# The scan of a state-space block: decay rows from a DRAM scratch instead of spreading products on TensorE

## The chip, the cores and the metric

The kernel runs on one core of a Trainium2 chip. The metric is the time of the whole kernel on the device, in microseconds (us). The median of three runs before the change is 1635.37 us (1634.31 to 1642.18).

## The reference, cut to what matters

The program is a transformer-like layer pair, then a second block whose mixer is a two-directional state-space scan (SSD), and a mixture of experts. The change touches only the scan of the second block. Sequence length is 256 and there are 32 heads of width 64, 4 groups, 128 states, 2 directions. For each head and direction:

```python
acs = jnp.cumsum(ac, axis=1)                     # running sum of the log decays
seg = acs[:, :, None] - acs[:, None, :]
decay = jnp.exp(jnp.where(lower, seg, -jnp.inf)) # 0 above the diagonal
cb = jnp.einsum('bign,bjgn->bijg', cc, bc)
y_diag = jnp.einsum('bijg,bijgr,bjgrp->bigrp', cb, decay, xc)
y_off = jnp.einsum('bign,bgrpn->bigrp', cc, state) * jnp.exp(acs)[..., None]
```

The kernel needs, for every head and direction, a tile in which each partition j holds the whole row acs[i] over i. To it the mask (0 or a large negative number) is added, acs[j] is subtracted as the bias of an exponential, and the result is multiplied by dt and by `cb`.

## The kernel before, in words

Every engine has its own program, written out by hand in its own order: `tensor` (PE), `scalar` (ACT), `vector` (DVE), `gpsimd` (POOL), `sync` (SP). Semaphores join them: `at(key)` names a point that another engine signals. All weights stream through a ring in SBUF. SP loads a *unit* (two column blocks of 512 KB); a unit is used as two *quarters*. For each quarter ACT makes a rounded high part (`hi_to`, 128x1024), POOL or DVE then the low part (`lo_to`), and PE multiplies high and low parts (three matmuls for each product). `split_done` says that PE has used a quarter up. In this part of the kernel the ring has two slots: before SP may load a unit it waits until both quarters of the unit two before it have their `hi` and `lo` (`load`, called by `load_to`).

The scan has 32 steps, `steps = [(c, d) ...]`: c is a pair of heads (0 to 15), d a direction; step n belongs to c = n // 2, d = n % 2. In the loop over n:

- PE: `spread(n + 2)`, `projected(n)` (the product of quarter n of the `merged` weights, 24 matmuls), `head_out(n)` (needs `mb` of step n), and in some steps `carried` (the state's part, in 12 of the steps) and `c_by_b`. `spread` makes the rows of two heads in PSUM: a product with a selection matrix (384 columns) and one with the identity that adds the mask (256 columns), for each of two heads.
- ACT: `hi_to(q0 + n + 4)`, which makes the high part of quarter n + 3; `exps(n + 2)`; at odd n `normed` (the last output's square and scaling); `gate_kept`.
- DVE: `weights_of(n + 1)` (four operations, signals `mb`); at even n `summed` and `gated`, at odd n `low`; then `carried`.
- POOL: `lo_to(q0 + n + 4)`; at odd n `squares`; sometimes a `carried` sum. All low parts of these quarters are POOL's.
- SP: nothing but units, each as early as the ring lets it. The unit with quarters n + 4 and n + 5 (n even) takes the slot of the unit with quarters n and n + 1.

The convolution ahead of the scan makes the running sums (`acs`), which PE transposes; ACT and DVE store them rounded as high and low parts (`ACSR`). ACT also makes a rounded copy of identity, selection matrix and masks (`KR`).

Of the kernel before, what the change touches and what calls it, by code (L numbers as in the profile page):

```python
# [6 lines left out]
F32 = mybir.dt.float32  # L7
F32R = mybir.dt.float32r
I32 = mybir.dt.int32
ALU = mybir.AluOpType  # L10
# [3 lines left out]
P = 128  # L14
D = 1024
# [16 lines left out]

CST = [("ident", 128), ("selh", 64), ("negf", 256), ("negb", 256), ("ones", 128), ("tle", 128), ("tge", 128), ("tlt", 128), ("tgt", 128),
       ("invf", 32), ("iota", 128), ("selbc", 128), ("selc", 2), ("half", 128)]
# [11 lines left out]
def constants():  # L46
# [6 lines left out]
    i = np.arange(256)[None, :]  # L53
    c["selh"] = p % 64 == np.arange(64)[None, :]
    c["negf"] = np.where(i % 128 >= p, 0.0, NEG)
# [236 lines left out]
def program(nc, A, out):  # L292
    st = ExitStack()
    with st:
# [35 lines left out]
        ar_r = rounded_at("arena_r", 25472, ar_at)  # L330
        acs_r = rounded_at("acs_r", 384, rows_at + 4 * 4 * D)
        ps = st.enter_context(nc.psum_tensor("ps", [P, 8, 512], F32))
# [39 lines left out]
        s_last = {e: sem(f"last_{e}") for e in ("dve", "pool")}  # L372
        s_w = [[sem(f"expert{i}") for i in range(9)]] + [[sem(f"expert{r}_{i}") for i in range(8)] for r in range(1, ROUNDS)]
        s_second = [sem(f"expert_second{i}") for i in range(4)]
        s_round = [None] + [{e: sem(f"round{r}_{e}") for e in ("pe", "act", "dve")} for r in range(1, ROUNDS)]
# [80 lines left out]
        AA = view(19712, 4, 64)  # L456
        ACS = view(19712, 2, 128)
        NACS = view(19968, 2, 64)
        WCE = view(20096, 4, 64)
        WC, EAC = WCE[:, 0:2, :], WCE[:, 2:4, :]  # L460
        ACSR = acs_r[:, :]
        H0T = XC
# [5 lines left out]

        KR = rounded_at("kr_r", 704, rows_at + 4 * 3 * D)[:, :]
        identr, selr, negr = KR[:, 0:128], KR[:, 128:192], [KR[:, 192:448], KR[:, 448:704]]  # L470
        SACC = view(17088, 1, 256)[:, 0, :]
        ED = [view(20480 + 768 * i, 2, 384) for i in range(3)]
        YO = [view(22784, 2, 512), view(23808, 2, 512)]
# [126 lines left out]
        def tensor(t):  # L600
# [346 lines left out]
            def convolution():  # L947
# [17 lines left out]
                for m in range(24):  # L965
# [16 lines left out]
                    if m == 11:  # L982
                        bk = take(("acst",), ("acsr", 0), ("acsr", 1))
                        t.wait_ge(*at("acs"))
                        for i in range(4):
                            made = t.transpose(bk[:, tok(i)], ACS[:, i % 2, :], ident)
                        made.then_inc(*sig(s_turn, ("acst_t",)))
# [58 lines left out]
            def scan():  # L1046
# [14 lines left out]

                def spread(n):
                    c, d = steps[n]
                    for e in range(2):
                        col = d * 32 + 2 * c + e
                        bk = take(("sp", n, e), ("ex", n, e))
                        t.wait_ge(*at("kr"))
                        t.wait_ge(*at("acsr", 0))
                        t.wait_ge(*at("acsr", 1))
                        t.matmul(bk[:, 0:384], selr[:, col:col + 1].to_broadcast([P, P]), ACSR, True, False)  # L1070
                        t.matmul(bk[:, parts_in[d][2]], identr, negr[d], False, True).then_inc(*sig(s_mm, ("sp", n, e)))

                def head_out(n):
# [7 lines left out]
                    for x, (cols, o) in enumerate(((early, slice(0, 256)), (late, slice(128, 256))) if d == 0 else ((late, slice(0, 256)), (early, slice(0, 128)))):  # L1081
                        for e in range(2):
                            h = 2 * c + e
                            made = t.matmul(bk[64 * e:64 * e + 64, o], XL[:, x if d == 0 else 1 - x, h * 64:h * 64 + 64], ED[n % 3][:, e, cols], d == 0 and x == 0, False)
                    made.then_inc(*sig(s_mm, ("ho", n)))
# [7 lines left out]
                    drop(("y", c))  # L1093

                c_by_b(0)
                spread(0)
                state_sum(3)
                for d in range(2):
                    for i in range(2):
                        carried(0, d, i)  # L1100
                    if d == 0:
                        spread(1)
                for n in range(32):
                    g, x = divmod(n, 8)
                    if x == 0 and g:
                        drop(("cb", g - 1))
                    if n + 2 < 32:
                        spread(n + 2)
                    if n >= 2:
                        projected(n)  # L1110
                    head_out(n)
                    if g < 3 and 2 <= x < 6:
                        carried(g + 1, *divmod(x - 2, 2))
                    if g < 3 and x == 6:
                        c_by_b(g + 1)
                drop(("cb", 3))

# [280 lines left out]
        def scalar(s):  # L1398
# [222 lines left out]
            def convolution():  # L1621
# [26 lines left out]
                for m in range(24):  # L1648
# [15 lines left out]
                    if m == 11:  # L1664
                        s.wait_ge(*at("acst_t"))
                        for z in range(4):
                            rs = slice(32 * z, 32 * z + 32)
                            made = s.activation(ACSR[rs, :], B("acst")[rs, 0:384] if z % 2 else B("acst")[rs, 128:512], ACT.Copy)
                        made.then_inc(*sig(s_act, ("acsr", 0)))
                    if m == 16:  # L1670
                        for h in range(2):
                            s.wait_ge(*at("ga", 3, 1, h))
                        s.wait_ge(*at("cst"))
                        s.activation(KR, cst[:, 0:704], ACT.Copy).then_inc(*sig(s_act, ("kr",)))
                    if m in KEPT:
# [20 lines left out]
            def scan():  # L1696
                q0 = first["merged",][1]
                def exps(n):
                    c, d = steps[n]
                    late, early, _ = parts_in[d]  # L1700
                    if n == 0:
                        s.wait_ge(*at("tk", CHUNKS.index(15)))
                    if n >= 3:
                        s.wait_ge(*at("ho", n - 3))
                    for e in range(2):
                        col = d * 32 + 2 * c + e
                        bk = B("sp", n, e)
                        s.wait_ge(*at("sp", n, e))
                        s.activation(ED[n % 3][:, e, late], bk[:, late], ACT.Exp, bias=NACS[:, 1, col:col + 1])
                        s.activation(ED[n % 3][:, e, early], bk[:, early], ACT.Exp, bias=NACS[:, 0, col:col + 1]).then_inc(*sig(s_act, ("ex", n, e)))  # L1710

# [175 lines left out]
        def vector(v):  # L1887
# [412 lines left out]
            def convolution():  # L2300
# [5 lines left out]
                for m in range(24):  # L2306
# [23 lines left out]
                    if m == 10:  # L2330
                        v.wait_ge(*at("wc"))
                        v.wait_ge(*at("dts"))
                        for i in range(2):
                            v.copy(ACS[:, :, 64 * i:64 * i + 64], fold(B("dts")[:, 128:256], 2))
                        then(v.tensor_scalar(NACS, fold(B("dts")[:, 128:256], 2), -1.0, None, ALU.mult), ("acs",))
                        v.wait_ge(*v.latest)
                        then(v.tensor_tensor(WC, WC, DT[:, 0:2, :], ALU.mult), ("wc", "made"))
                    if m == 11:
                        v.wait_ge(*at("acsr", 0))
                        for z in (2, 3):  # L2340
                            rs = slice(32 * z, 32 * z + 32)
                            made = v.tensor_tensor(ACSR[rs, :], B("acst")[rs, 0:384] if z % 2 else B("acst")[rs, 128:512], ACSR[rs, :], ALU.subtract)
                        then(made, ("acsr", 1))
                    if m == 13:
# [26 lines left out]
            def scan():  # L2371

                def weights_of(n):
                    c, d = steps[n]
# [3 lines left out]
                    for e in range(2):  # L2378
                        col = d * 32 + 2 * c + e
                        v.wait_ge(*at("ex", n, e))  # L2380
                        for z, cols, w in ((3, late, cb_in[d][0]), (2, early, cb_in[d][1])):
                            x = ED[n % 3][:, e, cols]
                            made = v.stt(x, x, DT[:, z, col:col + 1], bk[:, w], ALU.mult, ALU.mult)
# [28 lines left out]
                def low(c):  # L2412
                    v.wait_ge(*at("xsh", c))
                    then(v.stt(XSL[:, c, :], XST[:, c, :], ghalf[:, c:c + 1], xsh(c), ALU.mult, ALU.subtract), ("xsl", c))

                weights_of(0)
                state_kept(3)
                gated(0)
                for d in range(2):
                    for i in range(2):  # L2420
                        carried(0, d, i)
                for n, (c, d) in enumerate(steps):
                    g, x = divmod(n, 8)
                    lo_to(first["merged",][1] + n + 4)
                    if n + 1 < 32:
                        weights_of(n + 1)
# [536 lines left out]
        def sync(y):  # L2963
# [44 lines left out]
            for l in range(2):  # L3008
# [5 lines left out]
                for m, u in ADA_AT[l].items():  # L3014
# [3 lines left out]
                    y.wait_ge(*at("am", u))  # L3018
                load_to(first["z", 1, 1][0] if l == 0 else n1)
            load_to(first["end",][0])  # L3020
            y.wait_ge(*at("o2", 1, 1, "kept"))
# [77 lines left out]
```

## Time and profile before

| | |
|---|---|
| median of three runs | 1635.37 us |
| the profiled execution, span from first to last instruction | 1635.8 us |
| granted TensorE clock, mean | 0.995 |
| PE / DVE / ACT / POOL busy | 97% / 47% / 37% / 29% |
| scan, from PE's first loop step to its last product | about 860 to 1015 us |

The profile lists what each engine did when. PE is matmul time, DVE the vector engine, ACT the activation engine, POOL the GpSimd engine, SPq SP's queue of transfers. The mean times of matmuls overlap, because they are pipelined: what one costs is read from the distance between starts. The profiled execution's own time is its span, 1635.8 us; the page shows nothing around it.

### The profile page before, as it was taken

The numbers are of one execution on the slowest core, as the hardware profiler recorded it, in microseconds if no ns is written. First come the engines' busy times: TensorE is split into PE (matmuls) and PEld (weight loads), VectorE is DVE, ScalarE is ACT, GpSimd is POOL, SyncE is SP. The second block draws the span as 40 slices with busy tenths as digits, with TensorE's granted clock in tenths as the row PEclk, the third lists the DMA queues.
The fourth block names the chain that finished last, engine by engine and source line by source line (L and its number), as shares of the span: only waits on it lengthen the run. The fifth ranks groups of instructions, "written<-read, shape, count | busy, mean of one in ns | idle before, by whom it ended". The sixth has DMA issues, their size and how long they took to land.

```text
span 1635.8 us, 24320 instructions
## 1 busy us (share of the span) xinstructions
PE 1585.8 (97%) x9881; PEld 1204.8 (74%) x9881; DVE 762.6 (47%) x1261; ACT 611.0 (37%) x1113; POOL 473.7 (29%) x305
## 2 busy tenths in 40 slices
PE   6999999999999999999999999999999999999997
PEld 5988899878889998888778888898644444444442
DVE  4554433246454332578776666446532323333223
ACT  4644444345544443555446665333211111111010
POOL 4342655433434444300036665343300000000000
PEclk9999999999999999999999999999999999999998
DMA  7654997546439986433313333957999999999995
GB/s 264 220 158 128 266 260 232 174 141 218 153 98 312 263 269 220 118 80 85 103 52 104 104 103 120 296 152 264 360 400 423 425 420 422 424 422 424 421 422 210
DMA packets 244757, 397.87 MB, mean 243 GB/s; under 512 B 6837, under 2 KB 195697, under 8 KB 223392
## 3 DMA queue, kind: packets, MB, share of 16 engines
q1 hardware_dynamic: 237840, 365.45, 64.6%
q10 hardware_dynamic: 3776, 20.85, 3.2%
q0 software_dynamic: 3024, 9.95, 1.8%
q8 instruction: 81, 1.33, 0.3%
q14 instruction: 36, 0.29, 0.1%
HBM read 395.17 MB, written 1.05 MB: 242 GB/s over the span
## 4 chain that ended last, share of the span: by engine, by line
PE 82%; DMA 9%; DVE 3%; issue 2%; ACT 2%; POOL 1%; ACTq 0%; DVEq 0%; POOLq 0%; SPq 0%
PE ps L145 80%; DMA arena<-in_w_expert_up 4%; DMA arena<-in_w_expert_gate 4%; PE ps L147 2%; DVE arena L151 1%; DVE arena L155 1%; DMA ring<-in_w_out 1%; POOL split_r L151 1%; ACT arena L149 1%; DMA X<-in_x 1%; ACT split_r L149 1%; DVE split_r L151 0%; DMA ring<-in_w_in 0%; POOL arena_r L151 0%; DVE X L155 0%
## 5 line engine op out<-in xcount | busy, mean ns | idle before, releaser
L145 PE MATMUL ps<-arena_r,split_r 128*128 128x256 f32 (+1 forms) x2984 | 459.9, 288 | 2.2 <-POOL split_r L151 2.2
L151 POOL TENSOR_TENSOR split_r<-ring,split_r 128x1024 fp32r<-128x1024 f32 (+1 forms) x142 | 329.3, 2320 | 304.2 <-ACT split_r L149 275.6
L145 PEld LDWEIGHTS ps<-arena_r,split_r 128*128 128x128 f32 x2984 | 393.3, 188 | 19.7 <-issue 13.6
L149 ACT ACTIVATE split_r<-ring 128x1024 fp32r<-128x1024 f32 (+1 forms) x293 | 295.7, 1019 | 265.2 <-PE ps L145 183.2
L151 DVE TENSOR_TENSOR split_r<-ring,split_r 128x1024 fp32r<-128x1024 f32 (+1 forms) x151 | 217.4, 1442 | 302.6 <-ACT split_r L149 302.4
L145 PE MATMUL ps<-split_r,arena_r 128*128 128x512 f32 (+1 forms) x1520 | 341.0, 378 | 4.1 <-POOL split_r L151 2.4
L145 PEld LDWEIGHTS ps<-split_r,arena_r 128*128 128x128 f32 x1520 | 276.1, 189 | 50.3 <-issue 7.1
L145 PE MATMUL ps<-arena 128*64 128x512 f32 (+8 forms) x1456 | 299.1, 461 | 6.3 <-DMA arena<-in_w_expert_gate 2.2
L145 PE MATMUL ps<-hhh_r,split_r 128*128 128x256 f32 (+1 forms) x976 | 221.7, 316 | 0.0
L145 PEld LDWEIGHTS ps<-arena 128*64 128x64 f32 (+2 forms) x1456 | 126.0, 148 | 129.7 <-issue 115.2
L145 PE MATMUL ps<-ring,arena 128*64 128x512 f32 (+2 forms) x768 | 211.4, 576 | 3.0 <-DMA ring<-in_w_expert_up 1.7
L149 ACT ACTIVATE arena<-ps 128x256 f32<-128x256 f32 (+4 forms) x175 | 75.4, 446 | 257.3 <-PE ps L145 215.3
L145 PEld LDWEIGHTS ps<-hhh_r,split_r 128*128 128x128 f32 x976 | 161.6, 188 | 12.5 <-issue 0.6
L151 DVE TENSOR_TENSOR arena<-arena,ps 128x512 f32<-128x512 f32 (+1 forms) x120 | 72.7, 634 | 202.9 <-PE ps L145 177.3
L145 PEld LDWEIGHTS ps<-ring,arena 128*64 128x64 f32 (+1 forms) x768 | 77.3, 144 | 98.8 <-issue 89.4
L171 POOL DMA_DIRECT2D rows<-in_ln_g x1 | 0.6, 617 | 412.2 <-PE ps L145 412.2
L149 ACT ACTIVATE arena<-ps,modc 128x128 f32<-128x128 f32 x80 | 30.0, 455 | 199.2 <-PE ps L145 198.5
L149 ACT ACTIVATE arena_r<-arena 128x512 fp32r<-128x512 f32 (+2 forms) x96 | 51.0, 540 | 138.5 <-DVE arena L155 86.9
L145 PEld LDWEIGHTS ps<-arena,X 128*128 128x128 f32 x640 | 77.4, 198 | 28.5 <-issue 26.4
L145 PE MATMUL ps<-arena,X 128*128 128x128 f32 x640 | 82.6, 284 | 14.6 <-DVE arena L153 14.6
L155 DVE SCALAR_TENSOR_TENSOR arena<-ps,rows,arena 128x508 f32<-128x508 f32 (+4 forms) x104 | 69.7, 675 | 28.5 <-ACT arena L149 21.9
L151 POOL TENSOR_TENSOR arena_r<-arena,arena_r 128x256 fp32r<-128x256 f32 (+1 forms) x46 | 38.1, 830 | 151.3 <-ACT arena_r L149 143.7
(164 smaller groups left out, 1234.0 us busy)
## 6 DMA issues: line engine op xcount, KB each, us to landing
ring<-in_w_gate_up SPq DMA_DIRECT2D x88, 512.0 KB, 7.4
arena<-in_w_expert_gate SPq DMA_DIRECT2D x15, 2048.0 KB, 27.9
ring<-in_w_in SPq DMA_DIRECT2D x57, 512.0 KB, 5.3
ring<-in_w_expert_gate SPq DMA_DIRECT2D x13, 2048.0 KB, 25.7
ring<-in_w_expert_down SPq DMA_DIRECT2D x13, 2048.0 KB, 28.5
arena<-in_w_ada SPq DMA_DIRECT2D x24, 1024.0 KB, 7.4
arena<-in_w_expert_up SPq DMA_DIRECT2D x12, 2048.0 KB, 25.1
ring<-in_w_down SPq DMA_DIRECT2D x22, 1024.0 KB, 4.9
```

The costliest lines, as they stand in the source:

```text
L145: made = e.matmul(*a, **k)
L147: made = e.transpose(*a, **k)
L149: made = e.activation(*a, **k)
L151: made = e.tensor_tensor(*a, **k)
L155: made = e.scalar_tensor_tensor(**k)
L171: made = e.dma_start(*a, **k)
```

## The change

The running sums, transposed, are written once to a DRAM scratch `decays` of 64 rows of 384 numbers (`ACST`, 32-bit numbers, no rounding parts). For each step SP loads two of these rows onto all 128 partitions (3072 bytes a partition, 393 KB) into one of four buffers. DVE adds the mask, which PE has put into a PSUM bank once; ACT takes the exponential in place. `spread`, `KR`, `selh` and the parts of `ACSR` are gone. A fourth `ED` buffer lies in `rows`.

```diff
 # PE
-                def spread(n):            # per head: select product 384 columns, mask product 256
+                def masks():
+                    bk = take(("mask",), ("mk", 31), hold=True)
+                    t.matmul(bk[:, 0:256], ident, C("negf"), True, True)
+                    t.matmul(bk[:, 256:512], ident, C("negb"), True, True).then_inc(*sig(s_mm, ("mask",)))
+                masks()
                 c_by_b(0)
-                spread(0)
                 for n in range(32):
-                    if n + 2 < 32:
-                        spread(n + 2)
 # ACT, convolution step 11, and exps
-                        for z in range(4):
-                            rs = slice(32 * z, 32 * z + 32)
-                            made = s.activation(ACSR[rs, :], B("acst")[rs, 0:384] if z % 2 else B("acst")[rs, 128:512], ACT.Copy)
+                        for d in range(2):
+                            rs = slice(32 * d, 32 * d + 32)
+                            made = s.activation(ACST[rs, :], B("acst")[rs, 0:384] if d else B("acst")[rs, 128:512], ACT.Copy)
+                        made.then_inc(*sig(s_act, ("acst", "kept")))
+                        s.wait_ge(*s.latest)
+                        s.dma_start(DECAYS, ACST).then_inc(*landed(s_decays, ("decays_out",)))
-                        s.activation(KR, cst[:, 0:704], ACT.Copy).then_inc(*sig(s_act, ("kr",)))
-                    if n >= 3:
-                        s.wait_ge(*at("ho", n - 3))
+                    s.wait_ge(*at("mk", n))
 # DVE
+                def masked(n):
+                    _, d = steps[n]
+                    x = ED[n % 4][:, :, parts_in[d][2]]
+                    v.wait_ge(*at("mask"))
+                    v.wait_ge(*at("ed", n))
+                    then(v.tensor_tensor(x, x, B("mask")[:, 256 * d:256 * d + 256].unsqueeze(1).to_broadcast([P, 2, 256]), ALU.add), ("mk", n))
+                masked(0)
                 weights_of(0)
                 state_kept(3)
                 gated(0)
+                masked(1)
                 for n, (c, d) in enumerate(steps):
                     lo_to(first["merged",][1] + n + 4)
+                    if n + 2 < 32:
+                        masked(n + 2)
                     if n + 1 < 32:
                         weights_of(n + 1)
 # SP
+            def decays(n):
+                c, d = steps[n]
+                if n == 0:
+                    y.wait_ge(*at("decays_out"))
+                elif n < 4:
+                    y.wait_ge(*at("silu", 23))
+                    y.wait_ge(*at("tk", CHUNKS.index(15)))
+                else:
+                    y.wait_ge(*at("ho", n - 4))
+                two = DECAYS[32 * d + 2 * c:32 * d + 2 * c + 2, :].rearrange("a b -> (a b)")
+                y.dma_start(EDR[n % 4], two.partition_broadcast(P)).then_inc(*landed(s_ed[n % 4], ("ed", n)))
+
+            load_to(first["conv20",][0])
+            decays(0)
+            for n in range(1, 32):
+                load_to(first["merged",][0] + (n + 4) // 2 + 1)
+                decays(n)
             load_to(first["end",][0])
```

## Rows read from the trace of the kernel before

**Rows 1.** Busy time in a stretch; columns: stretch, PE, PEld, DVE, ACT, POOL, clock, DMA share, GB/s.

```profile
860.30:1014.50 154.20, 154.20 (x1195) 133.50 (x1193) 97.85 (x199) 93.42 (x212) 93.14 (x52) 1.00 0.40 110
...
1160.00:1165.00 5.00, 3.07 (x20) 2.91 (x21) 3.27 (x19) 0.20 (x1) 0.00 (x0) 0.82 1.01 423
```

**Rows 2.** Timeline of PE, one spread between a head's products and the next projection.

```profile
937.66 0.42 PE L145 MATMUL ps<-acs_r,kr_r 128*128 128x384 f32 x1
...
937.92 0.28 PE L145 MATMUL ps<-kr_r 128*128 128x256 f32 x1
...
938.04 0.33 PE L145 MATMUL ps<-acs_r,kr_r 128*128 128x384 f32 x1
...
938.21 0.28 PE L145 MATMUL ps<-kr_r 128*128 128x256 f32 x1
...
938.33 0.28 PE L145 MATMUL ps<-hhh_r,split_r 128*128 128x256 f32 x1
```

**Rows 3.** Timeline of PE: two `carried`; then the heads' products of steps 29 to 31.

```profile
858.95 1.88 PE L145 MATMUL ps<-arena 128*128 128x512 f32 x4
860.26 0.74 PE L145 MATMUL ps<-acs_r,kr_r 128*128 128x384 f32 x1
...
1005.51 0.87 PE L145 MATMUL ps<-arena 128*64 128x256 f32 x8
...
1009.79 0.87 PE L145 MATMUL ps<-arena 128*64 128x256 f32 x8
1013.63 0.87 PE L145 MATMUL ps<-arena 128*64 128x256 f32 x8
1014.43 0.71 PE L145 MATMUL ps<-cst_sb,arena 128*128 128x128 f32 x4
```

**Rows 4.** Timeline of ACT, two steps: gate, high part, exponentials, square, scaling, gate, high part.

```profile
895.13 0.47 ACT L149 ACTIVATE arena<-ps,stat 128x256 f32<-128x256 f32 x1 [1.00 <-PE ps L145]
...
901.34 1.36 ACT L149 ACTIVATE arena<-ps,arena 128x256 f32<-128x256 f32 x4
902.57 0.43 ACT L149 ACTIVATE arena<-arena 128x256 f32<-128x256 f32 x1
902.87 0.52 ACT L149 ACTIVATE arena_r<-arena,stat 128x256 fp32r<-128x256 f32 x1
904.39 0.47 ACT L149 ACTIVATE arena<-ps,stat 128x256 f32<-128x256 f32 x1 [1.00 <-PE ps L145]
904.76 1.05 ACT L149 ACTIVATE split_r<-ring 128x1024 fp32r<-128x1024 f32 x1
```

**Rows 5.** Timeline of POOL: low parts; the first at the scan's start, the second in it.

```profile
856.69 2.36 POOL L151 TENSOR_TENSOR split_r<-ring,split_r 128x1024 fp32r<-128x1024 f32 x1 [5.86 <-ACT split_r L149]
...
896.63 2.40 POOL L151 TENSOR_TENSOR split_r<-ring,split_r 128x1024 fp32r<-128x1024 f32 x1 [2.08 <-ACT split_r L149]
```

**Rows 6.** SP's queue: issues of one unit (the second line from a later start), and their landing.

```profile
899.11 0.99 SPq L171 DMA_DIRECT2D ring<-in_w_in  x2
...
899.52 0.58 SPq L171 DMA_DIRECT2D ring<-in_w_in  x1
...
DMA to landing us min/median/max: 4.2/5.2/6.1
```

**Rows 7.** SP's waits ahead of its transfers between 850 and 1010 us.

```profile
SPq L138 <- ACT split_r L149: 112.3, 16, 15.8
SPq L138 <- POOL split_r L151: 36.6, 15, 2.6
```

**Rows 8.** Timeline of DVE in an even step: weights, sum, gating product, gate.

```profile
904.00 1.38 DVE L155 SCALAR_TENSOR_TENSOR arena<-arena,ps 128x256 f32<-128x256 f32 x4
905.84 0.48 DVE L155 SCALAR_TENSOR_TENSOR arena<-arena,stat,ps 128x256 f32<-128x256 f32 x1 [0.46 <-PE ps L145]
906.35 2.22 DVE L151 TENSOR_TENSOR arena<-arena 128x256 f32<-128x256 f32 x1
909.66 0.42 DVE L155 SCALAR_TENSOR_TENSOR arena<-arena,ps 128x256 f32<-128x256 f32 x1 [1.09 <-ACT arena L149]
```

**Rows 9.** DVE's two-input additions and products in the scan; ns min/median/max, first and last start.

```profile
L151 DVE TENSOR_TENSOR arena<-ps,arena x14: 690/692/694, 860.0 to 969.2; 128x512 f32<-128x512 f32 x14
L151 DVE TENSOR_TENSOR arena<-arena x14: 425/2214/2622, 865.9 to 998.3; 128x256 f32<-128x256 f32 x14
```

**Rows 10.** The page: a queue's packets, MB and share; transfers, count, KB, us to landing.

```profile
q0 software_dynamic: 3024, 9.95, 1.8%
...
rows<-in_g_mix_post POOLq DMA_DIRECT2D x2, 512.0 KB, 5.0
...
out<-arena SPq DMA_DIRECT2D x4, 256.0 KB, 2.3
```

More of the change, by code:

```diff
@@ L31 @@
 C1, C2, C3 = 6.25, 0.033185303211212158203125, 3.9683743e-09
-CST = [("ident", 128), ("selh", 64), ("negf", 256), ("negb", 256), ("ones", 128), ("tle", 128), ("tge", 128), ("tlt", 128), ("tgt", 128),
+CST = [("ident", 128), ("negf", 256), ("negb", 256), ("ones", 128), ("tle", 128), ("tge", 128), ("tlt", 128), ("tgt", 128),
        ("invf", 32), ("iota", 128), ("selbc", 128), ("selc", 2), ("half", 128)]
@@ L53, in constants @@
     i = np.arange(256)[None, :]
-    c["selh"] = p % 64 == np.arange(64)[None, :]
     c["negf"] = np.where(i % 128 >= p, 0.0, NEG)
@@ L330, in program @@
         ar_r = rounded_at("arena_r", 25472, ar_at)
-        acs_r = rounded_at("acs_r", 384, rows_at + 4 * 4 * D)
         ps = st.enter_context(nc.psum_tensor("ps", [P, 8, 512], F32))
@@ L373, in program @@
         s_w = [[sem(f"expert{i}") for i in range(9)]] + [[sem(f"expert{r}_{i}") for i in range(8)] for r in range(1, ROUNDS)]
+        s_decays, s_ed = sem("decays_out"), [sem(f"decay{i}_in") for i in range(4)]
         s_second = [sem(f"expert_second{i}") for i in range(4)]
@@ L456, in program @@
         AA = view(19712, 4, 64)
-        ACS = view(19712, 2, 128)
+        ACS = view(19712, 2, 64)
         NACS = view(19968, 2, 64)
@@ L460, in program @@
         WC, EAC = WCE[:, 0:2, :], WCE[:, 2:4, :]
-        ACSR = acs_r[:, :]
+        ACST = rows[0:64, 4 * D:4 * D + 384]
         H0T = XC
@@ L467, in program @@
         XW = view(24576, 2, 2, 512)
-        KR = rounded_at("kr_r", 704, rows_at + 4 * 3 * D)[:, :]
-        identr, selr, negr = KR[:, 0:128], KR[:, 128:192], [KR[:, 192:448], KR[:, 448:704]]
+        DECAYS = nc.dram_tensor("decays", (64, 384), F32).ap()
         SACC = view(17088, 1, 256)[:, 0, :]
-        ED = [view(20480 + 768 * i, 2, 384) for i in range(3)]
+        EDR = [view(20480 + 768 * i, 1, 768)[:, 0, :] for i in range(3)] + [rows[:, 2 * D:2 * D + 768]]
+        ED = [fold(x, 2) for x in EDR]
         YO = [view(22784, 2, 512), view(23808, 2, 512)]
@@ L982, in convolution @@
                     if m == 11:
-                        bk = take(("acst",), ("acsr", 0), ("acsr", 1))
+                        bk = take(("acst",), ("acst", "kept"))
                         t.wait_ge(*at("acs"))
                         for i in range(4):
-                            made = t.transpose(bk[:, tok(i)], ACS[:, i % 2, :], ident)
+                            made = t.transpose(bk[0:64, tok(i)], ACS[:, i % 2, :], ident)
                         made.then_inc(*sig(s_turn, ("acst_t",)))
@@ L1060, in carried @@
                     t.matmul(bk, CT[:, g, tok(i)], H0T[:, d, half(g)], True, True).then_inc(*sig(s_mm, ("yo", g, d, i)))
-                def spread(n):
[L1063 to L1071, printed above, removed]
+                def masks():
+                    bk = take(("mask",), ("mk", 31), hold=True)
+                    t.matmul(bk[:, 0:256], ident, C("negf"), True, True)
+                    t.matmul(bk[:, 256:512], ident, C("negb"), True, True).then_inc(*sig(s_mm, ("mask",)))
                 def head_out(n):
@@ L1083, in head_out @@
                             h = 2 * c + e
-                            made = t.matmul(bk[64 * e:64 * e + 64, o], XL[:, x if d == 0 else 1 - x, h * 64:h * 64 + 64], ED[n % 3][:, e, cols], d == 0 and x == 0, False)
+                            made = t.matmul(bk[64 * e:64 * e + 64, o], XL[:, x if d == 0 else 1 - x, h * 64:h * 64 + 64], ED[n % 4][:, e, cols], d == 0 and x == 0, False)
                     made.then_inc(*sig(s_mm, ("ho", n)))
@@ L1100, in scan @@
                         carried(0, d, i)
-                    if d == 0:
-                        spread(1)
                 for n in range(32):
@@ L1115, in scan @@
                         c_by_b(g + 1)
-                drop(("cb", 3))
+                drop(("cb", 3), ("mask",))
             def two_chunks(n, key, free, src):
@@ L1665, in convolution @@
                         s.wait_ge(*at("acst_t"))
-                        for z in range(4):
-                            rs = slice(32 * z, 32 * z + 32)
-                            made = s.activation(ACSR[rs, :], B("acst")[rs, 0:384] if z % 2 else B("acst")[rs, 128:512], ACT.Copy)
[L1669 to L1673, printed above, removed]
-                        s.activation(KR, cst[:, 0:704], ACT.Copy).then_inc(*sig(s_act, ("kr",)))
+                        for d in range(2):
[4 more added lines that the diff above has]
+                        s.dma_start(DECAYS, ACST).then_inc(*landed(s_decays, ("decays_out",)))
                     if m in KEPT:
@@ L1700, in exps @@
                     late, early, _ = parts_in[d]
-                    if n == 0:
-                        s.wait_ge(*at("tk", CHUNKS.index(15)))
-                    if n >= 3:
-                        s.wait_ge(*at("ho", n - 3))
+                    x = ED[n % 4]
+                    s.wait_ge(*at("mk", n))
                     for e in range(2):
                         col = d * 32 + 2 * c + e
[L1707 to L1710, printed above, removed]
+                        s.activation(x[:, e, late], x[:, e, late], ACT.Exp, bias=NACS[:, 1, col:col + 1])
+                        s.activation(x[:, e, early], x[:, e, early], ACT.Exp, bias=NACS[:, 0, col:col + 1]).then_inc(*sig(s_act, ("ex", n, e)))
                 def normed(c):
@@ L2332, in convolution @@
                         v.wait_ge(*at("dts"))
-                        for i in range(2):
-                            v.copy(ACS[:, :, 64 * i:64 * i + 64], fold(B("dts")[:, 128:256], 2))
+                        v.copy(ACS, fold(B("dts")[:, 128:256], 2))
                         then(v.tensor_scalar(NACS, fold(B("dts")[:, 128:256], 2), -1.0, None, ALU.mult), ("acs",))
@@ L2337, in convolution @@
                         then(v.tensor_tensor(WC, WC, DT[:, 0:2, :], ALU.mult), ("wc", "made"))
[L2338 to L2343, printed above, removed]
                     if m == 13:
@@ L2381, in weights_of @@
                         for z, cols, w in ((3, late, cb_in[d][0]), (2, early, cb_in[d][1])):
-                            x = ED[n % 3][:, e, cols]
+                            x = ED[n % 4][:, e, cols]
                             made = v.stt(x, x, DT[:, z, col:col + 1], bk[:, w], ALU.mult, ALU.mult)
```

## The prediction

> **What bounds the kernel now.** I read the busy times by stretch first. In the scan PE is busy for all of its 154.2 us, DVE for 97.9, ACT for 93.4 and POOL for 93.1, and the DMA engines are busy 40% [rows 1]. So PE sets the pace, and everything that PE need not do there looks like a gain. The timelines give the pace: two steps take 9.26 us (the same gate operation starts at 895.13 and at 904.39 [rows 4]). Then I read the queues that the change adds to. What matters is not how busy they are but in which order they stand. After PE finishes a projection, ACT makes the high part of the quarter four later, POOL its low part (896.63 to 899.03 [rows 5]), and only then SP issues the next unit, at 899.11 [rows 6]. SP's waits are all of this kind: high or low parts of the unit before the last, 149 us in 31 waits [rows 7]. Today nobody minds, because SP carries only weights, which are needed two steps later.
>
> **What the change removes.** A spread takes from 937.66 to 938.33 on PE, 0.67 us between starts. 0.09 of it (the first 0.26 against 0.17 for the same product later) is the step out of the head's products, which stays [rows 2]. That leaves 0.58 us x 32 = 18.6 us. The last two steps, which have no spread today, confirm it: 4.28 + 3.84 = 8.12 us for two [rows 3], against 9.26, so 1.14 a pair. If nothing else came to bound, the kernel would take 1635.8 - 18.6 = 1617 us. In the convolution four copies, two subtractions and the copy of the constants go, one transfer comes. They lie beside PE's matmuls; I take 0 (at most a few tenths). `masks` replaces the first spread on PE; I take 0.
>
> **What it adds on DVE.** One addition of 2 x 256 columns from SBUF and PSUM a step. The nearest row has the same engine, the same number of elements and one PSUM operand: 0.69 us, without spread over 14 [rows 9]. That is 22 us on an engine with 56 us to spare. The additions whose two inputs are both in SBUF take 0.43 to 2.62 us [rows 9], as those that meet POOL's work do; the mask is in PSUM, so I take 0.69 and not 2.2. By busy time alone DVE does not become the bound (98 + 22 = 120 us against PE's 136).
>
> **What it adds on SP, and the wait behind it.** This decides. For even n, SP's order is: the unit with quarters n + 4 and n + 5, then `decays(n)`, then `decays(n + 1)`. That unit needs the low part of quarter n + 1. ACT makes the high part of this quarter at the head of its loop step n - 2, directly in front of `exps(n)`; and `exps(n)` needs the very rows that SP may fetch only afterwards. DVE waits for them in its step n - 2 too, in `masked(n)`, with `weights_of(n - 1)` queued behind it, for which PE waits in `head_out(n - 1)`. The four buffers do not help, since the wait in SP's queue, not the buffer, holds the load back. So there is a ring from `masked(n)` to `masked(n + 2)`, once for two steps. Its links, with M the end of `masked(n)`:
>
> DVE: `weights_of(n - 1)` 1.38, `summed` 0.48 and 0.43 (the lower end, because POOL is not at work yet), `gated` 0.42 [rows 8, 9], `masked(n + 1)` 0.69, gaps 0.1: 3.5 us. ACT was up to `exps(n)`, a gate and a high part meanwhile (1.36 + 0.4 + 1.05 = 2.8) and does not hold it up. ACT: `exps(n + 1)`, square, scaling, gate, high part of quarter n + 3: 1.23 + 0.30 + 0.52 + 0.37 + 1.05 = 3.5 [rows 4]: M + 7.0. POOL: 0.08 to start, 2.40 for the low part [rows 5]: M + 9.5. SP: 0.08 until it issues; the second half of the unit lands 6.1 us after its own issue, at 905.6, 6.6 us after the low part's end [rows 5, 6]. `decays(n + 2)` stands behind it in the same queue. Its 393 KB, at the rate of POOL's row transfers (9.95 MB in 1.8% of 16 x 1635.8 us is 338 GB/s [rows 10]), take 1.16 us more: 7.75. With 0.05 to wake DVE and `masked(n + 2)`, 8.5. The ring takes 18.0 us for two steps, against PE's 8.12. Where DVE's `carried` (0.69 [rows 9]) stands in an even step, six times, it is that much longer.
>
> **The cost of the transfer, from both sides.** No row shows this transfer. If it overtook the unit, it would land like the store of 256 KB, 2.3 us after issue [rows 10], plus 0.4 for the greater size; issued 1.4 us after the low part (two issues of the unit and its own [rows 6]), 4.1 in place of 7.75: a ring of 14.4. If it started only when the unit has landed and took the 5.0 us of a 512 KB row transfer [rows 10], 11.6: a ring of 21.9. I take 7.75, because the two halves of one unit land one after the other, at 903.3 and 905.6 [rows 6], so the queue goes roughly in order.
>
> On this the Trainium skill says the same: in "DMA: Bandwidth & Descriptors", section "Queues, rings and completion order", each engine consumes its descriptors in ring order; by that too the transfer stands behind the unit. Its fit (section "Anatomy of one DMA", 2.0 us and bytes / 436 GB/s) would, as an estimate, give 2.9 us for the transfer alone; as it adds only 0.9 behind the unit, the ring would be 17.7 us and the total 4 us less. No row here shows such a transfer alone.
>
> **The sum.** The low part of quarter 3 ends at 859.05 [rows 5]; nothing ahead of it changes. `masked(2)` ends 8.5 later, at 867.6. The first ring has no `summed`, no `gated`, no `normed` and no gate: DVE reaches `masked(3)` 2.1 after M, ACT ends `exps(2)`, high part 4, `exps(3)`, high part 5 at 4.8, POOL low parts 4 and 5 (one after the other) at 7.4, then 8.5: 15.9. `masked(4)` ends at 883.5. Then 13 rings x 18.0 and 6 x 0.69: `masked(30)` at 1121.6. `weights_of(29)` and the wake add 1.5: PE starts `head_out(29)` at 1123.1. Today it starts at 1005.5 [rows 3], and from there on the work is the same. So +117.6 us, and 1635.8 + 117.6 = 1753 us. The profiled execution (1635.8) and the median (1635.37) agree within 0.03%, so the number stands for both. The 18.6 us are in it: PE does not have the spreads, it only waits longer.
>
> **Rivals.**
>
> *PE stays the bound, 1617 us (faster).* This holds if the rows of step n are in place before DVE asks for them, which needs a ring of at most 8.12 us. For it speaks PE's 100% [rows 1] and the 60% of DMA time that is free. Against it: DVE, ACT and POOL links alone are 9.5 us, before any byte moves. The gain needs my reading of the order to be wrong. 5%.
>
> *The ring is partly hidden, 1632 to 1700.* For instance the rows might be fetched a unit earlier than I read, and only DVE's and ACT's queues lengthen. With a ring of 9.3 the time is as before; beyond this each us costs 14 us. 7%, of which 3% within 0.5% of before.
>
> *The rows come slowly.* 128 partitions read the same 3 KB, or the two steps' rows share the rate: +1.2 to +3.9 us a ring, 1770 to 1807. The row transfers of the first block land in 5.0 us beside streams [rows 10], which speaks against the worst. 13%.
>
> *PE loses its clock.* In the one stretch with PE busy 3.07 of 5 us the granted clock was 0.82, between the levels of 1.2 and 2.4 GHz [rows 1]. In the scan after the change PE would be busy about half of the time. At 1.2 GHz its 8.12 us become 16.2, still under 18.0; pairs with two `carried` (0.65 us each, from 858.95 to 860.26 for two [rows 3]; twice that at the lower clock) reach 18.8. PE would add some 5 us in the scan and 8 at its end: 1766. 15%.
>
> The Trainium skill ("TensorE: Matmul & The Clock Gate", section "HAM oscillation") has the rule that waits for data in each turn of a loop make the array fall back to its slow clock every time. By it this rival happens.
>
> **How the numbers follow.** The ring as computed: 60%, 1753, own range 1725 to 1770. With the slow rows 13%, the clock 15%, partly hidden 7%, faster 5%. The bounds of the transfer give 1753 - 14 x 3.65 = 1702 and 1753 + 14 x 3.9 = 1807; the range 1700 to 1807 leaves out the last two cases. About 0.5% (8 us) is what a measurement tells from no change. Faster 0.05, same 0.03, slower 0.92.
>
> **What would show it.** In the profile after: PE busy about half in the scan, which ends near 1130 us in place of 1015; the same gate operation every 18 us, not 9.3; DVE idle until the rows' transfer, some 7 us in each pair of steps; a transfer of 384 KB issued right behind each second unit and landing about 6 us later; DVE's mask additions at 0.69 us. No matmul on `kr_r`. The experts' part unchanged, only later. I am wrong if SP issues `decays(n)` before POOL's low part of quarter n + 1 ends, if pairs take under 14 us, or if DVE never waits on a DMA.

## The result

The change makes the kernel slower. The median goes from 1636.26 us to 1744.70 us (four runs each, 1740.07 to 1751.57 after); the ratio is 1.0655 with a 95% interval of 1.0632 to 1.0678. The prediction was 1753 us, range 1700 to 1807. The profiled execution has a span of 1738.3 us, 102.5 more than before; it belongs to the shortest of the four runs.

Busy time of the scan after, same columns as [rows 1]:

```profile
860.00:1125.00 265.00, 177.04 (x1093) 145.95 (x1090) 100.68 (x232) 97.06 (x215) 92.12 (x54) 0.79 0.36 108
```

PE, 100% busy in 154 us before, is now busy 177 of 265 us, and the granted clock is 0.79. DVE, ACT and POOL do about the same work as before. Who waits for whom in this stretch (waiting engine and tile, releaser, total us, times, longest):

```profile
POOL split_r L150 <- ACT split_r L148: 168.0, 26, 12.5
ACT arena L148 <- DVE arena L150: 161.9, 23, 12.1
DVE arena L150 <- DMA arena<-decays: 147.7, 15, 13.0
...
PE ps L144 <- DVE arena L154: 51.0, 8, 7.8
...
PE ps L144 <- DVE rows L154: 36.9, 7, 5.9
```

Each engine in the loop waits for the one ahead of it, and the last in the row waits for the transfer of the decays' rows: 147.7 us in 15 waits, one for each even step from 2. SP's own waits (850 to 1120 us) close the circle:

```profile
SPq L137 <- ACT split_r L148: 186.6, 16, 13.9
SPq L137 <- POOL split_r L150: 36.2, 15, 2.4
```

The chain of waits that ended last shows the ring itself, from one even step's mask addition (935.07) to the next (951.89). Columns are start, us, what:

```profile
935.07 0.69 DVE arena L150
935.75 1.70 DVE arena L154 x5
937.46 0.02 issue
937.48 0.42 DVE arena L150
937.90 0.33 DVE arena L154
938.24 0.61 DVE rows L150
938.84 0.02 issue
938.87 1.49 ACT rows L148 x4
940.36 0.31 ACT arena L148
940.67 0.40 ACT arena_r L148
941.07 0.36 ACT arena L148
941.42 0.96 ACT split_r L148
942.38 0.07 issue
942.45 2.38 POOL split_r L150
944.83 0.02 issue
944.85 0.03 SPq L137
944.87 0.03 issue
944.90 0.38 SPq L170
945.29 0.04 issue
945.33 0.58 SPq L170
945.91 0.04 issue
945.96 5.91 DMA arena<-decays
951.87 0.02 issue
951.89 0.69 DVE arena L150
```

The links of the prediction stand there in their order: mask addition of the even step, weights, sum, product, gate and the odd step's mask addition on DVE; exponentials, square, scaling, gate and high part on ACT; low part on POOL; two issues of a unit on SP (944.90, 945.33); then the rows' transfer. PE is nowhere in it. It is 16.8 us long. The mask additions of the even steps recur at this pace through the whole scan (DVE's timeline, the first and the last of 15, 14 rings apart: 17.2 us each):

```profile
865.90 0.69 DVE L150 TENSOR_TENSOR arena<-arena,ps 128x512 f32<-128x512 f32 x1 [5.79 <-DMA arena<-decays]
...
1107.06 0.69 DVE L150 TENSOR_TENSOR arena<-arena,ps 128x512 f32<-128x512 f32 x1 [9.81 <-DMA arena<-decays]
```

The scan's last products, as in [rows 3] (first and last line):

```profile
1109.11 1.55 PE L144 MATMUL ps<-arena 128*64 128x256 f32 x8 [6.95 <-DVE arena L154]
...
1119.74 0.71 PE L144 MATMUL ps<-cst_sb,arena 128*128 128x128 f32 x4
```

The scan ends at 1120.5, 105.3 us later than before (1015.1). The rest of the kernel is 2.8 us shorter in this execution. The four runs of the changed kernel lie up to 11.5 us apart, so a difference of this size can't be told from their spread, and it stays open.

From the first of these products to the last line the scan takes 11.3 us, where it took 9.6 before (1005.51 to 1015.14 [rows 3]). Here PE's clock is on the path, for after the last ring PE waits for nothing any more. It comes out of a wait of 6.95 us, and the granted clock of the next 5 us is 0.61 on average, near the lower of its two levels (1.2 and 2.4 GHz):

```profile
1109.00:1114.00 5.00, 4.89 (x28) 4.19 (x29) 3.92 (x10) 4.62 (x11) 3.08 (x2) 0.61 0.00 0
```

The same eight products that start the tail take 1.55 us in the trace, and 0.87 before. These 1.7 us, once, are what the lower clock costs in this trace.

### The profile page after: what moved, and what is told of

Its sections match the earlier page's. It is cut to its first block, busy times and chain, and to the rows that moved or that the text cites. A ratio compares the mean times of both kernels' runs of the same rounds, so it can differ in the third digit from the quotient of the medians.

```text
span 1738.3 us, 24083 instructions
## 1 busy us (share of the span) xinstructions
PE 1603.1 (92%) x9757; PEld 1212.6 (70%) x9757; DVE 764.5 (44%) x1290; ACT 611.0 (35%) x1110; POOL 471.3 (27%) x305
## 4 chain that ended last, share of the span: by engine, by line
PE 74%; DMA 14%; DVE 6%; POOL 2%; ACT 2%; issue 1%; SPq 0%; ACTq 0%; DVEq 0%; POOLq 0%
PE ps L144 72%; DMA arena<-decays 5%; DMA arena<-in_w_expert_up 4%; DMA arena<-in_w_expert_gate 4%; PE ps L146 2%; DVE arena L150 2%; DVE arena L154 2%; POOL split_r L150 2%; ACT arena L148 1%; ACT split_r L148 1%; DMA X<-in_x 1%; DVE rows L154 1%; DVE split_r L150 1%; DMA ring<-in_w_in 0%; POOL arena_r L150 0%
## 5 line engine op out<-in xcount | busy, mean ns | idle before, releaser
L144 PE MATMUL ps<-arena_r,split_r 128*128 128x256 f32 (+1 forms) x2984 | 465.9, 290 | 3.2 <-POOL split_r L150 3.2
L144 PEld LDWEIGHTS ps<-arena_r,split_r 128*128 128x128 f32 x2984 | 400.4, 191 | 25.3 <-issue 19.8
L144 PE MATMUL ps<-hhh_r,split_r 128*128 128x256 f32 (+1 forms) x976 | 243.9, 338 | 0.0
L150 DVE TENSOR_TENSOR arena<-arena,ps 128x512 f32<-128x512 f32 (+1 forms) x144 | 89.1, 643 | 350.1 <-PE ps L144 176.8
L144 PEld LDWEIGHTS ps<-hhh_r,split_r 128*128 128x128 f32 x976 | 173.8, 203 | 18.0 <-issue 6.0
L144 PE MATMUL ps<-rows,arena 128*64 128x512 f32 (+2 forms) x224 | 82.4, 572 | 38.1 <-DVE rows L154 36.9
L148 ACT ACTIVATE arena<-arena 128x128 f32<-128x128 f32 (+3 forms) x119 | 45.4, 443 | 173.8 <-DVE arena L150 169.6
```

The source lines that it names most:

```text
L144: made = e.matmul(*a, **k)
L148: made = e.activation(*a, **k)
L150: made = e.tensor_tensor(*a, **k)
```

## The experiments

e1, e2 and e5 do the changed kernel's own work in another order. e4 and e7 add transfers, e3 and e6 matmuls, whose results nobody reads. Each diff is against the changed kernel, where nothing else is said. Ratios are against the kernel before, run on the same chip; the changed kernel itself was not run again beside the experiments. A difference of a few us between the medians of two kernels lies within the intervals (about 4 us each way), and single traces differ more.

**e1: rows ahead of the unit in SP's queue.**

```diff
-            for n in range(1, 32):
-                load_to(first["merged",][0] + (n + 4) // 2 + 1)
-                decays(n)
+            load_to(first["merged",][0] + 3)
+            decays(1)
+            for n in range(2, 32, 2):
+                decays(n)
+                decays(n + 1)
+                load_to(first["merged",][0] + n // 2 + 3)
```

> The changed kernel with one edit: in SP's queue the rows of steps n and n + 1 (n even) stand ahead of the unit with quarters n + 4 and n + 5, not behind it. Same transfers, same bytes, same work on all engines. Theory (the ring through SP's queue): the rows are then issued as soon as the head's products four steps back are done, the ring is cut, PE is the bound again without its spreads: 1617 us, up to 1632 if DVE, now with the mask additions, holds PE up in some steps; pairs of steps of 8.1 to 9 us. Rival 1 (the 12.6 MB of row transfers or their latency are what costs): same traffic, so about 1740. Rival 2 (DVE's additions or the in-place exponentials lengthen the step): about 1740 too. Rival 3 (PE's lower clock is the cost): the clock comes back only if the waits go, so it does not differ from the theory here.

Measured: 1619.28 us against 1637.78, ratio 0.9892 (0.9867 to 0.9917). The whole loss is gone and the gain from the missing spreads is there: 18.5 us between these medians, where 18.6 were computed. The same bytes move, and the same additions and exponentials are made. Busy time in the scan of e1, columns as above:

```profile
860.00:1000.00 140.00, 138.20 (x1072) 118.02 (x1073) 98.69 (x229) 96.41 (x212) 91.58 (x52) 0.99 0.67 199
```

PE is busy 138.2 of 140 us again, while DMA moves 199 GB/s, nearly twice what it moves in the slow scan. DVE still waits for rows, but less (between 860 and 1120 us), and PE hardly notices: it waits for DVE once, near the start (860 to 1000 us, second line).

```profile
DVE arena L150 <- DMA arena<-decays: 17.1, 10, 3.7
...
PE ps L144 <- DVE arena L154: 1.9, 1, 1.9
```

The scan's last product, as above:

```profile
998.59 0.71 PE L144 MATMUL ps<-cst_sb,arena 128*128 128x128 f32 x4
```

The scan ends at 999.3, 15.8 us earlier than before. The profiled execution as a whole is 20.1 us shorter (1615.7 against 1635.8); the 4.3 us behind the scan are of the size by which runs of one kernel differ.

**e2: only the even step's rows ahead of the unit** (diff against e1).

```diff
             for n in range(2, 32, 2):
                 decays(n)
-                decays(n + 1)
                 load_to(first["merged",][0] + n // 2 + 3)
+                decays(n + 1)
```

> The changed kernel with half of that edit: rows of step n (even) ahead of the unit, rows of step n + 1 still behind it. Theory: a ring remains, but through the odd step: mask addition of n + 1, exponentials 1.5, square, scaling and gate 1.1, high part of quarter n + 3 1.05, POOL 2.5, unit and rows 7.1, mask addition 0.7: 13.9 us for two steps in place of the 17.2 measured, so 14 x 3.3 = 47 us less than the changed kernel: about 1693 us. Rivals of traffic or of DVE's work: about 1740, since nothing is taken out. If any early issue is enough: about 1620.

Measured: 1694.76 us, ratio 1.0351 (1.0323 to 1.0379), 2 us from the number expected. The ring now goes through the odd steps. Their first and last mask addition on DVE, 14 rings apart (14.2 us each, 13.9 expected):

```profile
866.20 0.69 DVE L150 TENSOR_TENSOR rows<-rows,ps 128x512 f32<-128x512 f32 x1 [3.81 <-DMA rows<-decays]
...
1064.53 0.69 DVE L150 TENSOR_TENSOR rows<-rows,ps 128x512 f32<-128x512 f32 x1 [5.67 <-DMA rows<-decays]
```

So it is not enough to issue some rows early: each transfer that a later link waits for must be out of the ring.

**e5: another link taken out, SP's queue as in the changed kernel.** ACT and POOL make their parts of a quarter one step earlier.

```diff
 # ACT
-                    hi_to(q0 + n + 4)
+                    hi_to(q0 + n + 5)
 # POOL
-                lo_to(q0 + n + 4)
+                lo_to(q0 + n + 5)
```

> The changed kernel with SP's queue left as it is. Only ACT's and POOL's order is changed: each makes the split parts of quarter n + 4, not n + 3, at the head of its step n, so the high part of quarter n + 3 no longer stands behind the exponentials, square and scaling of step n + 1. Theory: the links of the ring from DVE's second mask addition through ACT's exponentials go out of it; it becomes exponentials 1.5, gate 0.3, high part 1.05, POOL 2.45, unit and rows 7.1, mask addition 0.7 = 13.1 us in place of 17.2, 14 times: 57 us less than the changed kernel, about 1688 us. Rival (the wait for the transfers alone sets the pair, whatever ACT does): about 1745.

Measured: 1680.65 us, ratio 1.0265 (1.0240 to 1.0290), 64 us less than the changed kernel, 7 more than expected. The even steps' mask additions on DVE, 13 rings apart (13.4 us each, 13.1 expected):

```profile
879.90 0.69 DVE L150 TENSOR_TENSOR arena<-arena,ps 128x512 f32<-128x512 f32 x1 [9.59 <-DMA arena<-decays]
...
1053.60 0.69 DVE L150 TENSOR_TENSOR arena<-arena,ps 128x512 f32<-128x512 f32 x1 [6.61 <-DMA arena<-decays]
```

The transfers and their place in SP's queue are untouched, and yet the pair gets 3.9 us shorter. Over 14 rings that is 54 us, and the two profiled executions differ by just that (1738.3 and 1684.7); the rest of the 64 is within the spread of the runs. A wait for the transfers alone could not do this; a ring in which ACT's work is a link does.

**e4: one more transfer in the ring**, and **e7: the same transfers with the ring cut.** Both have this edit, e7 on top of e1. Left out here are the new semaphore and a wait for the last of these transfers, both in SP's program behind the scan's loads.

```diff
+                if n >= 4 and n % 2 == 0:
+                    if n > 4:
+                        y.wait_ge(*at("extra", n - 2))
+                    y.dma_start(rows[:, 2816:3584], two.partition_broadcast(P)).then_inc(*landed(s_extra, ("extra", n)))
                 y.dma_start(EDR[n % 4], two.partition_broadcast(P)).then_inc(*landed(s_ed[n % 4], ("ed", n)))
```

> The changed kernel with one more transfer of the same kind (two rows onto all partitions, 393 KB, into memory that nobody reads) between each unit and the rows of even steps from 4 (14 of them). Theory: the transfers of a queue move their bytes in the order of the queue, so each ring grows by the transfer's own 1.2 us, plus 0.4 for its issue if that is not hidden: 14 x 1.2 = +16 us against the changed kernel (up to +22). If only fixed latency counted and the bytes were free: 0. If bandwidth for rows read by 128 partitions were the loss (some 4 us a transfer): +50.

Measured: 1763.18 us, ratio 1.0761 (1.0735 to 1.0788), 18.5 us more than the changed kernel for 14 transfers: 1.3 us for each. In e4's trace the even steps' mask additions are 14 rings apart at

```profile
867.12 0.69 DVE L150 TENSOR_TENSOR arena<-arena,ps 128x512 f32<-128x512 f32 x1 [5.69 <-DMA arena<-decays]
...
1133.55 0.69 DVE L150 TENSOR_TENSOR arena<-arena,ps 128x512 f32<-128x512 f32 x1 [10.59 <-DMA arena<-decays]
```

which is 19.0 us each, 1.8 more than in the changed kernel. This trace is of e4's longest run and that one of the changed kernel's shortest, so 1.3 and 1.8 are the two readings that there are; expected were 1.2 to 1.6. Both say that bytes ahead in the queue count with about their own time, not with a latency of some 4 us.

> The kernel of e1 (rows ahead of the unit) with the 14 further transfers of 393 KB of e4, each ahead of the rows of its even step. Theory: with the ring cut, the bytes lie beside PE's work; 1619 us as e1, or up to 1630 where the rows now land too late for a step. Rival (each transfer on this queue costs its time wherever it stands): 18 us more than e1, 1637, as e4 against the changed kernel.

Measured: 1623.29 us, ratio 0.9918 (0.9896 to 0.9941), 4 us more than e1, not 18. DVE's waits for rows grow (860 to 1000 us), and PE waits for DVE three times, once in e1:

```profile
DVE arena L150 <- DMA arena<-decays: 30.6, 14, 3.7
...
PE ps L144 <- DVE rows L154: 2.5, 2, 2.0
PE ps L144 <- DVE arena L154: 1.9, 1, 1.9
```

By the medians the same 5.5 MB cost 18.5 us in the ring and 4 outside it.

**e3 and e6: PE's clock held up.** Matmuls that nobody needs, 30 or 16 of them, fill PE's wait in odd steps.

```diff
+                    if n >= 3 and n % 2:
+                        bk = take(("over", "scan", n))
+                        for _ in range(30):   # 16 in e6
+                            t.matmul(bk[:, 0:P], ident, ones, True, True)
                     head_out(n)
```

> The changed kernel with 30 more matmuls (identity by ones, 128 columns, into a bank that nobody reads) ahead of the head's products in each odd step from 3, where PE now waits for DVE some 6 us; their results are not used. Theory (ring): PE does not stand in the ring, so pairs stay at 17.2 us although the granted clock goes from 0.79 to near 1.0; the total stays within 5 us of the changed kernel (1738 to 1745). Rival (the lower clock is a real part of the loss): 5 to 15 us faster than the changed kernel. If the fill is too long in some pairs it shows as up to 5 us slower.

> The changed kernel with 16 more matmuls (3.7 us at the full clock) ahead of the head's products in odd steps, not 30: short enough that PE still waits for DVE afterwards. Theory: 1740 to 1746, that is the same as the changed kernel, less at most 5 us at the scan's end if the clock stays up. Rival (the lower clock is a real part of the loss): 1730 to 1738.

Measured: e3 1748.59 us, ratio 1.0679 (1.0657 to 1.0701); e6 1743.11 us, ratio 1.0649 (1.0628 to 1.0670). The clock of the scan rises from 0.79 to 0.95 in e3 and to 0.89 in e6. Busy times of the scan, first e3, then e6:

```profile
860.00:1125.00 265.00, 241.19 (x1920) 219.29 (x1919) 100.31 (x230) 95.23 (x215) 91.65 (x53) 0.95 0.36 109
```

```profile
860.00:1125.00 265.00, 209.54 (x1539) 184.67 (x1538) 100.16 (x231) 96.21 (x216) 92.00 (x53) 0.89 0.36 109
```

Neither is faster than the changed kernel beyond the intervals. e3 is 3.6 us above the range that was expected (1738 to 1745), within the 5 us that the expectation allowed for a fill that is too long; e6 is where it was expected. The pace of the rings shows it without the spread of the runs. In e6 the even steps' mask additions are 14 rings apart at

```profile
868.10 0.69 DVE L150 TENSOR_TENSOR arena<-arena,ps 128x512 f32<-128x512 f32 x1 [6.04 <-DMA arena<-decays]
...
1110.85 0.69 DVE L150 TENSOR_TENSOR arena<-arena,ps 128x512 f32<-128x512 f32 x1 [9.54 <-DMA arena<-decays]
```

so 17.3 us each; in e3 (868.51 to 1111.55) it is 17.4, in the changed kernel 17.2. The clock rises and the ring stays as it is. In e3 the fill is too long in some pairs: DVE's `carried` additions now wait for PE four times (between 860 and 1120 us), which they never do in the changed kernel.

```profile
DVE arena L150 <- PE ps L144: 21.3, 4, 6.7
```

The totals of e3 and e6 can't price the 1.7 us at the scan's end. Step 31 has a fill too, and nothing is left to wait for there, so the fill itself lies on PE's path: from 1122.45 to 1126.11 in e6, 3.7 us, and 6.8 us in e3.

```profile
1122.45 3.73 PE L144 MATMUL ps<-cst_sb 128*128 128x128 f32 x32
```

So the lower clock is a consequence of the waits and costs nothing inside the rings. Behind them the changed kernel's trace has its 1.7 us, out of 105.

## Why the prediction was right

*The order in SP's queue decides.* Shown three ways: by the chain, which in the pair shown has every predicted link and no other, by e1, which cuts the ring with nothing but the order, and by e2 and e5, which move the ring or shorten it and land at 14.2 and 13.4 us where 13.9 and 13.1 were expected.

*The size of the ring.* 18.0 us was predicted, 16.8 measured between 935.07 and 951.89. With the steps that have `carried` and the shorter first ring the prediction had 18.1 on average over 14 rings, and 17.2 was measured. Two terms were too large. DVE's link from M to the end of `masked(n + 1)` was put at 3.5 and is 3.1 (935.76 to 938.84): neighbouring operations overlap by about 0.1 us, and I had added their full durations. The rows landed 7.75 us after the low part's end by the prediction and did so after 7.04 (944.83 to 951.87). Most of this is the unit and not the rows: its second half, issued at 945.33, landed 5.5 us after its issue, where the one unit that the prediction read took 6.1.

```profile
L170 SPq DMA_DIRECT2D ring<-in_w_in x1: 584/584/584, 945.3 to 945.3; - x1
...
DMA to landing us min/median/max: 5.5/5.5/5.5
```

Why it landed sooner no run shows. The rows then landed 1.0 us behind it, where 1.16 was put. In the last 2 us before that landing the queue moved 0.70 MB, 351 GB/s, so the rate of 338 GB/s taken from POOL's transfers [rows 10] was near. The one row transfer of the scan that had nothing ahead of it (issued at 847.85) landed 3.3 us after its issue; 2.7 was the prediction's bound for it, and 2.9 its estimate from the Trainium skill, whose fit ("DMA: Bandwidth & Descriptors", section "Anatomy of one DMA") is stated for transfers that GpSimd issues, while SP issues these.

*From 1753 to the profiled 1738.3.* `masked(2)` began at 865.9, not 866.9: 1.0 us. The 14 rings are 12.9 us shorter in sum: the first was longer than predicted (16.9 against 15.9), the other 13 took 17.25 each where 18.3 was predicted with `carried`. The stretch from `masked(30)` to `head_out(29)` is 0.1 shorter. The scan's tail at the lower clock is 1.7 longer, where the prediction had no change, and the part behind the scan is 2.8 shorter. Together 15.1 us, which is the distance to 1753.4 (1635.8 + 117.6).

*Two of the signs were off in size.* PE is busy 177 of 265 us in the scan, two thirds and not half; at a granted clock of 0.79 its matmuls take longer. DVE waits for rows some 10 us in each pair (147.7 us in 15 waits), not 7. Neither is a term of the sum.

*The saving of the spreads.* 18.6 us were computed; they appear only when the ring is cut (e1: 18.5 us between the medians, 15.8 at the scan's end in the trace, where PE still waits for a moment). In the changed kernel they are bought and lost in a wait.

*DVE's additions* took 0.69 us as taken from [rows 9], also beside POOL's work (in e1 the one at 865.68 lies wholly within POOL's low parts, 863.00 to 867.73), and DVE did not become the bound: 98.7 of 140 us in e1.

*The rival of slow rows* falls: the rows landed 1.0 us behind the unit, and each added transfer cost 1.3 to 1.8 us (e4). *The rival of the clock* was right about the clock, 0.79, and wrong about its price: it had 5 us in the scan and 8 at its end, and the runs show none in the rings (e3, e6) and 1.7 at the end. The rule of the Trainium skill ("TensorE: Matmul & The Clock Gate", section "HAM oscillation"), that waits in each turn of a loop bring the slow clock, agrees with the 0.79. Here PE is no link of the ring, and all that the slow clock costs is the 1.7 us behind it. *The faster rival's* time is e1's: it needed one edit of the order, which the change did not have.

## What to carry to other kernels

Before a load is put into a queue, ask of each entry ahead of it what that entry waits for, and follow this back: if the path comes to the reader of the load, buffers do not help, and the loop runs at the length of the ring, whatever the busy times say. Here the new loads stood behind weights that waited for split parts made behind the loads' own readers; with the two exchanged the change gains 1.1% in place of losing 6.6%. A load whose buffer comes free early belongs ahead of one whose buffer comes free late.

## What the runs showed of the hardware that was not expected

DVE's product with both inputs in SBUF took 0.42 us where POOL stood still (937.48 in the chain) and has a median of 2.21 us before [rows 9]. The timelines of DVE and POOL, laid side by side, show when it is short. Before, four of the scan's 15 products had no POOL operation beside them; they took 0.42 or 0.43 us, and each of the other 11 took the time that it shared with POOL's addition and 0.27 to 0.29 us more. In the changed kernel the 14 products of the rings meet no POOL operation, and all take 0.42 or 0.43. So the ring happened to free DVE from meeting POOL's work. DVE's additions with an input in PSUM take 0.69 us in either case. Not every meeting costs: in e2 three products took 0.42 to 0.47 us though POOL was at work all the while, and why is open.

SP's issue of the first row transfer behind a unit took 1.25 us, against 0.34 for one with nothing ahead (its queue in the changed kernel):

```profile
847.85 0.34 SPq L170 DMA_DIRECT2D arena<-decays  x1
...
945.96 1.25 SPq L170 DMA_DIRECT2D arena<-decays  x1
```

The second row transfer, right behind the first, took 0.43 us, so the two are 1.7 us of SP for this unit. Whether the long issue delays the landing no run shows; other work of SP it did not hold up, because SP had none.
